# Second half of x turned inside the q/k product, two up units in side buffers, and the last y in another bank

## The chip, the core and the metric

One core of a Trainium2 chip runs the kernel. The metric is the device time of one execution in microseconds (us). The engines are TensorE (PE; PEld is its weight load), VectorE (DVE), ScalarE (ACT), GpSimd (POOL) and SyncE (SP). SyncE and ScalarE each issue transfers on a DMA queue of their own (q1 and q10 in the profile).

## The reference, cut to what matters

Two layers over 256 tokens of width 1024, all in float32. Layer 0 mixes with an mLSTM, layer 1 with windowed attention; each is followed by a grouped top-2 mixture of 16 experts and by layer norms.

```
proj = x @ w_in                      # q, k (512 each), v, o (1024 each), gates (2 x 4)
gates = 15 * tanh((gates + b_gates) / 15)
h = mlstm(q, k, v, gates) ; h = norm(h) * mh_norm * sigmoid(o) ; mix = h @ w_out
x = LN(alpha * x + mix)
for e in range(16):                  # moe, gate is zero but for the token's two experts
    g, u = split(t @ w_gu[e])        # 1024 -> 2 x 512
    out += gate[:, e] * ((silu(g) * u) @ w_down[e])
x = LN(alpha * x + out)
...                                  # layer 1: q, k, v, attention, w_out, LN, the same moe, LN
```

## The kernel before, in words

**Engines.** Every engine has its own program, written out in order; they meet only at semaphores. An instruction or a DMA issue that waits holds up everything behind it on its engine.

**Weights.** All large weights are streamed through `ring`, 22 slots of 1 MB ("units": 256 rows of a matrix, two a partition). Unit i goes into slot i modulo 22. SyncE issues the loads in the order of use; the load of unit i waits until `freed`, a counter that TensorE raises after its last use of each unit, has reached i - 21 (`free_slot`). TensorE waits for the slot's own counter (`need`). The q and k weights are units 0 to 3, then four each of v, o and w_out. From unit 16 on stand layer 0's experts: four up units (`u_gu`) and two down units (`u_dn`) each, in the order up(0), up(1), down(0), up(2), down(1) and so on; then the keys and values, q, w_out and the experts of layer 1.

**The start.** SyncE issues the first half of x's columns for both token tiles (two DMAs), unit 0, the second half of x (two DMAs), then units 1 and on. TensorE turns x in 128 x 128 blocks (`turn`, four blocks a call): both tiles of the first half (j=0), then both of the second (j=1). The copies of the results from PSUM to `hT` are divided: VectorE takes tile 1 of the first half, ScalarE the other three, in the order (tile 0, j 0), (tile 0, j 1), (tile 1, j 1). Then TensorE makes q and k transposed in one product, k = 0 to 7, with eight matmul instructions each (16 in the records, as each float32 matmul shows twice) into banks 0 to 3; k = 0 to 3 read the first half of x, k = 4 to 7 the second. Then come the gate product, which waits for `gates_w_in`, and the four V projections.

ScalarE loads the small parameters on its own queue, in its program order:

```
for t, j, n in ((0, 0, 1), (0, 1, 3), (1, 1, 4)):
    act.wait_ge(turned, n)
    A(hT[...], pb[4 + 2 * t + j]..., ACT.Copy).then_inc(hT_act, 1)
gate_weights()                       # four loads of w_in's gate columns, two of b_gates
act.dma_start(rows[0][0:4], ...)     # ln_g, ln_b, mh_norm, then w_rt x2, b_rt, sink x2, cs x2
...
for g in range(8):                   # only then q and k are copied out of PSUM, and the tanh follows
```

Each of the four loads of the gate columns moves 512 pieces of 16 bytes (four columns of 512 rows), each of the two bias loads four numbers. `gates_w_in` counts to 96 when all six are there; VectorE waits for it too, for its small operation on `b_gate` (in tile `misc`).

**The experts.** For expert u in `ORDER`, TensorE's `gate_up(u)` makes 64 token slots times 1024 columns in bank 0: 8 k steps of two matmul instructions, raising `freed` after each second k. ScalarE applies silu, VectorE multiplies and turns the result in 32 x 32 blocks (`turn_inner`, eight transposes) into `heT`. `down(u)` multiplies it by the two down units into bank 2, which VectorE and ScalarE must have emptied of the y before (`take_y`, counters `y_sb`). The order is gate_up(u+1), down(u), gate_up(u+2), down(u+1) and so on, with gathers (`gather`) and scatters (`scatter`) of tokens between for each quad of experts. The last quad ends: gate_up(15), down(14), a turn of the gate table (`turn_table`), down(15), scatter, layer norm.

Tile `bufA` holds the output gates of the mLSTM, the probabilities in layer 1, and in the experts the y of a quad, from the first `take_y` on. Tile `hT` holds turned activations, is read last before the experts by the routing product (which raises `logits`), and becomes the gathered tokens of the second quad.

Of the kernel before, what the change touches and what calls it, by code (L numbers as in the profile page):

```python
# [11 lines left out]
SEQ, D = 256, 1024  # L12
P = 128
NT = SEQ // P
# [23 lines left out]
TAKEN = 2.0e30  # L38
RING = 22
U_QK, U_V, U_O, U_WO = 0, 4, 8, 12  # L40
U_MOE = [16, 122]
U_KV, U_Q, U_WOB = 112, 114, 118


def u_gu(l, u):
    return U_MOE[l] + (6 * u - 2 if u else 0)


def u_dn(l, u):
    return U_MOE[l] + (6 * u + 8 if u < EXPERTS - 1 else 94)  # L50


def build(nc, x, w_in_a, b_gates_a, mh_norm_a, w_out_a, w_kv_shared, w_q_b, sinks_b, w_out_b,
          w_router, b_router, w_gu, w_down, ln_g, ln_b, rope, out):
    ctx = ExitStack()
    with ctx:
# [51 lines left out]
        probT = [bufA[:, 1024 + n * 512:1024 + (n + 1) * 512] for n in range(2)]  # L108

        res = gate_o  # L110
        ln_row = [bufB[:, n * D:(n + 1) * D] for n in range(2)]

        xe = [bufB[:, :].rearrange("p (k s) -> p k s", k=KC), hT]
# [42 lines left out]

        ring_in = [sem(f"ring_in{n}") for n in range(RING)]
        freed = sem("freed")
        x_in = [[sem(f"x_in{j}{t}") for t in range(NT)] for j in range(2)]
        gates_w_in, params_in = sem("gates_w_in"), sem("params_in")  # L160
        rows_in, rows_part, rows_ready = sem("rows_in"), sem("rows_part"), sem("rows_ready")
# [56 lines left out]
            return START + 14 * l + (4 * m - 2 if m else 0)  # L218


        SCB = [[[0, 1], [4, 5]], [[2, 3], [6, 7]]]
        SC_ORDER = [(t, par, jj) for t in range(NT) for jj in range(2) for par in range(2)]

        @block.sync
        def _(sp):
            def free_slot(i):

                if i >= RING:
                    sp.wait_ge(freed, i - RING + 1)
                if i == U_KV + RING:  # L230
                    sp.wait_ge(qT_done, 4)

            def load(i0, src):

                v = src.rearrange("(q p j) n -> p q j n", p=P, j=2)
                for q in range(src.shape[0] // 256):
                    buf, got = slot(i0 + q)
                    free_slot(i0 + q)
                    sp.dma_start(buf[:, :, :], v[:, q]).then_inc(got, 16)

            def load_down(i0, src):

                v = src.rearrange("(p q j) n -> p q j n", q=2, j=2)
                for q in range(2):
                    buf, got = slot(i0 + q)
                    free_slot(i0 + q)
                    sp.dma_start(buf[:, :, :], v[:, q]).then_inc(got, 16)

            def load_by_head(i0, src):

                v = src.rearrange("(k p) n -> p k n", p=P)
                for q in range(4):
                    buf, got = slot(i0 + q)
                    free_slot(i0 + q)
                    sp.dma_start(buf[:, :, :], v[:, 2 * q:2 * q + 2, :]).then_inc(got, 16)

            def spill(l):

                s = ov[l]
                sp.wait_ge(lists, l + 1)  # L260
                rounds = sp.value_load(extra[0:1, l:l + 1], min_val=0, max_val=3)
                with sp.If(rounds > 0):
                    sp.wait_ge(s["dve"], 1)
                    with sp.Fori(0, rounds) as j:
                        with sp.Fori(0, EXPERTS) as e:
                            n0 = (j * EXPERTS + e) * (KC + FC)
                            for k in range(KC + FC):

                                sp.wait_ge(s["w_used"], n0 + (k + START))
                                kk = k if k < KC else k - KC  # L270
                                if k < KC:
                                    src = w_gu[l, bass.ds(e, 1), kk // 2 * 256:(kk // 2 + 1) * 256, :].rearrange(
                                        "a (p j) n -> j (a p) n", j=2)[kk % 2]
                                else:
                                    src = w_down[l, bass.ds(e, 1), :, :].rearrange("a (p k) n -> k (a p) n", k=FC)[kk]
                                sp.dma_start(spill_w, src).then_inc(s["w_in"], 16)

            def load_x(j):

                for t in range(NT):  # L280
                    sp.dma_start(h[:, t, j * HALF:(j + 1) * HALF], x[0, t * P:(t + 1) * P, j * HALF:(j + 1) * HALF]).then_inc(x_in[j][t], 16)
            w_in = w_in_a[0]
            load_x(0)
            load(U_QK, w_in[0:256, 0:1024])
            load_x(1)
            load(U_QK + 1, w_in[256:1024, 0:1024])
            load(U_V, w_in[:, 1024:2048])
            load(U_O, w_in[:, 2048:3072])
            load(U_WO, w_out_a[0])
            load(u_gu(0, 0), w_gu[0, ORDER[0]])  # L290
            for l in range(2):
                for n, src in enumerate((ln_g, ln_b)):
                    sp.dma_start(norm_col[:, l, n, :].rearrange("p (a j) -> p a j", j=2),
                                 src[l, 0].rearrange("(a p j) -> p a j", p=P, j=2)).then_inc(cols_in, 16)
            for u in range(EXPERTS):
                if u + 1 < EXPERTS:
                    load(u_gu(0, u + 1), w_gu[0, ORDER[u + 1]])
                load_down(u_dn(0, u), w_down[0, ORDER[u]])
            for q in range(2):
                buf, got = slot(U_KV + q)  # L300
                free_slot(U_KV + q)
                sp.dma_start(buf[:, :, :].rearrange("p a (b n) -> p (a b) n", b=2).rearrange("p (a j) n -> p a j n", j=2),
                             w_kv_shared.rearrange("(a p j) n -> p a j n", p=P, j=2)[:, 2 * q:2 * q + 2]).then_inc(got, 16)
            load(U_Q, w_q_b[0])
            load_by_head(U_WOB, w_out_b[0])
            load(u_gu(1, 0), w_gu[1, ORDER[0]])
            load(u_gu(1, 1), w_gu[1, ORDER[1]])
            load_down(u_dn(1, 0), w_down[1, ORDER[0]])
            spill(0)
            for u in range(1, EXPERTS):  # L310
                if u + 1 < EXPERTS:
                    load(u_gu(1, u + 1), w_gu[1, ORDER[u + 1]])
                load_down(u_dn(1, u), w_down[1, ORDER[u]])
            spill(1)

            for t in range(NT):
                for c in range(2):
                    sp.wait_ge(ln_ready, 2 * (3 * NT + t) + c + 1)
                    sp.dma_start(out[0, t * P:(t + 1) * P, c * HALF:(c + 1) * HALF],
                                 h[:, t, c * HALF:(c + 1) * HALF]).then_inc(stored, 16)  # L320
            sp.wait_ge(stored, 16 * 2 * NT)
# [54 lines left out]
        def _(pe):  # L376
# [95 lines left out]


            pe.wait_ge(consts, NCONST)
            for j in range(2):
                for t in range(NT):
                    pe.wait_ge(x_in[j][t], 16)
                    turn(h, 0, t, j, 4)
            for k in range(KC):
                if k % 2 == 0:  # L480
                    need(U_QK + k // 2)
                if k % 4 == 0:
# [83 lines left out]
            def moe(l):  # L566
# [51 lines left out]
                def gate_up(u):  # L618
# [3 lines left out]
                    for k in range(KC):  # L622
                        if u and g == 0 and k == 4:
                            turn_table(m - 1)
                        if k % 2 == 0:
                            need(u_gu(l, u) + k // 2)
                        if g == 0 and k % 4 == 0:

# [5 lines left out]
                        for c in range(2):  # L634
                            last = mm(pb[0][c * 64:(c + 1) * 64, :].rearrange("p (a n) -> p a n", a=2),  # L635
                                      xe[m % 2][:, k, g * SLOTS:(g + 1) * SLOTS],
                                      slot(u_gu(l, u) + k // 2)[0][:, k % 2, :]
                                      .rearrange("p (a c n) -> p c a n", a=2, c=2)[:, c],
                                      start=k == 0, stop=k == KC - 1)
                        if k % 2:  # L640
                            last.then_inc(freed, 1)

                def turn_table(m):
# [8 lines left out]

                def down(u):
                    pe.wait_ge(heT_sb, E0 + (u + 1))
                    for t in range(NT):
                        pe.wait_ge(y_sb[t], (E0 + u) * 2 - START)
                    for hf in range(2):
                        w = slot(u_dn(l, u) + hf)[0]
                        need(u_dn(l, u) + hf)
                        for j in range(2):  # L660
                            for c in range(2):
                                last = mm(pb[2][c * 64:(c + 1) * 64, :],  # L662
                                          heT[u == EXPERTS - 1][:, (2 * hf + j) * 64:(2 * hf + j + 1) * 64],
                                          w[:, j, c * HALF:(c + 1) * HALF],
                                          start=(j, hf) == (0, 0), stop=(j, hf) == (1, 1))
# [222 lines left out]
        def _(act):  # L888
# [108 lines left out]
            def moe(l):  # L997
# [15 lines left out]
                def take_y(u):  # L1013
# [2 lines left out]
                    act.wait_ge(freed, u_dn(l, u) + 2)  # L1016
                    for t in range(NT):
                        A(ye[t][g * BLOCK:(g + 1) * BLOCK, HALF:2 * HALF],  # L1018
                          pb[2][64 + t * BLOCK:64 + (t + 1) * BLOCK, :], ACT.Copy).then_inc(y_sb[t], 1)

                def silu(u):
                    act.wait_ge(freed, u_gu(l, u) + 4)
                    A(act_g[u % 2], pb[0][:, 0:256], ACT.Silu).then_inc(silu_done, 1)  # L1023

                take_x(0, 0, 3)
# [101 lines left out]
        def _(dve):  # L1127
# [283 lines left out]
            def experts(l):  # L1411
# [16 lines left out]
                def take_y(u):  # L1428
# [2 lines left out]
                    dve.wait_ge(freed, u_dn(l, u) + 2)  # L1431
                    for t in range(NT):
                        V.tensor_copy(ye[t][g * BLOCK:(g + 1) * BLOCK, 0:HALF],  # L1433
                                      pb[2][t * BLOCK:(t + 1) * BLOCK, :]).then_inc(y_sb[t], 1)

                make_pick(0).then_inc(pick_ready, 1)
                V.reduce_max(extra_f[:, 0:1], pb[1][:, 32:64], AX_X)
# [229 lines left out]
```

## Time and profile before

| | |
|---|---|
| median of 3 runs | 689.04 us (688.61 to 690.35) |
| the profiled execution | 691.68 us, of which the span is 690.0 us |
| TensorE matmul, busy | 655.5 us (95%) |
| VectorE, busy | 284.3 us (41%) |
| ScalarE, busy | 139.7 us (20%) |
| bytes moved | 231.43 MB, mean 335 GB/s |
| chain that ended last | PE 81%, DMA 9%, DVE 5%, ACT 2% |

The profile is of one execution. Times in it count from the start of its span. A busy share is a mean over stages with different limits: the DMA engines are full for the first 86 us and during the experts (421 GB/s) and nearly idle between.

### The profile page before, as it was taken

The page shows a single profiled execution, that of the slowest core. Times are in us where ns is not written, and L with a number is a line of the kernel's source. Part 1 is how long each engine was busy: PE and PEld are TensorE (multiplying, and loading weights), DVE is VectorE, ACT ScalarE, POOL GpSimd, SP SyncE. Part 2 cuts the span into 40 slices and gives each one's busy share as a digit, 9 for nine tenths or more (in the row PEclk, how much of TensorE's full clock was granted, in tenths as well). Part 3 has the DMA queues.
Part 4 walks back from the last instruction along what each step waited for, and adds up shares of the span by engine and source line. Part 5 has one row for each costly group of instructions (what it writes and reads, how often), then busy time and mean ns, then how long its engine had stood idle before and what let it go on. Part 6 is the DMA issues. An engine that isn't in the chain of part 4 may idle for free.

```text
span 690.0 us, 7113 instructions
## 1 busy us (share of the span) xinstructions
PE 655.5 (95%) x2746; PEld 292.3 (42%) x2746; DVE 284.3 (41%) x730; ACT 139.7 (20%) x321; POOL 22.6 (3%) x41
## 2 busy tenths in 40 slices
PE   5999999999999999999979998999999999999974
PEld 4854564465333333333324454546333333333321
DVE  0001303256535335253445344456553444435356
ACT  1003234021121121121222042312021121021212
POOL 2040100000000000000000011200000000000000
PEclk9999999998999999999999999999999999999998
DMA  8999903261999999999999980823899999999991
GB/s 318 388 405 348 425 17 134 110 237 58 417 421 422 420 421 422 422 421 421 419 417 414 421 337 9 359 101 144 326 423 422 420 421 420 423 419 423 419 389 64
DMA packets 41431, 231.43 MB, mean 335 GB/s; under 512 B 10153, under 2 KB 10153, under 8 KB 15794
## 3 DMA queue, kind: packets, MB, share of 16 engines
q1 hardware_dynamic: 36960, 230.72, 81.7%
q10 hardware_dynamic: 4434, 0.21, 0.4%
q8 instruction: 24, 0.39, 0.2%
q14 instruction: 13, 0.11, 0.0%
HBM read 229.87 MB, written 1.05 MB: 335 GB/s over the span
## 4 chain that ended last, share of the span: by engine, by line
PE 81%; DMA 9%; DVE 5%; ACT 2%; SPq 1%; POOL 1%; issue 1%; POOLq 0%; DVEq 0%; ACTq 0%
PE pb L635 28%; PE pb L435 16%; PE pb L662 14%; DMA ring<-in_w_down 8%; PE pb L487 4%; PE pb L682 3%; PE pb L789 2%; PE pb L613 2%; PE pb L391 1%; PE pb L615 1%; PE pb L398 1%; PE pb L409 1%; DMA h<-in_x 1%; PE pb L538 1%; PE pb L579 1%; POOL bufA L372 1%
## 5 line engine op out<-in xcount | busy, mean ns | idle before, releaser
L435 PE MATMUL pb<-ring,hT 128*128 128x512 f32 x320 | 141.7, 595 | 0.8 <-DVE hT L1619 0.8
L662 PE MATMUL pb<-ring,bufC 128*64 128x512 f32 x512 | 117.0, 597 | 4.9 <-DVE bufA L1433 2.7
L635 PE MATMUL pb<-ring,hT 128*64 128x512 f32 x512 | 114.6, 594 | 2.0 <-DMA ring<-in_w_gu 2.0
L635 PE MATMUL pb<-ring,bufB 128*64 128x512 f32 x512 | 113.2, 593 | 0.0
L1407 DVE STREAM_TRANSPOSE bufC<-bufC 32x128 f32<-32x128 f32 x256 | 102.9, 402 | 3.8
L1433 DVE COPY bufA<-pb 32x512 f32<-32x512 f32 x64 | 43.7, 682 | 122.9 <-PE pb L662 121.9
L435 PEld LDWEIGHTS pb<-ring,hT 128*128 128x128 f32 x320 | 59.3, 190 | 69.7 <-issue 67.7
L635 PEld LDWEIGHTS pb<-ring,hT 128*64 128x64 f32 x512 | 36.0, 137 | 75.0 <-issue 68.0
L635 PEld LDWEIGHTS pb<-ring,bufB 128*64 128x64 f32 x512 | 36.2, 137 | 71.8 <-issue 70.0
L662 PEld LDWEIGHTS pb<-ring,bufC 128*64 128x64 f32 x512 | 35.0, 136 | 72.7 <-issue 68.1
L1018 ACT ACTIVATE bufA<-pb 32x512 f32<-32x512 f32 x64 | 37.7, 589 | 115.9 <-PE pb L662 115.1
L1023 ACT ACTIVATE bufC<-pb 128x256 f32<-128x256 f32 x32 | 12.3, 383 | 192.3 <-PE pb L635 192.3
L1416 DVE TENSOR_TENSOR bufC<-bufC,pb 128x256 f32<-128x256 f32 x32 | 13.5, 421 | 81.5 <-ACT bufC L1023 81.5
L682 PE MATMUL pb<-bufA,v_shift 128*128 128x512 f32 x64 | 29.5, 604 | 1.7 <-DVE bufA L1433 1.7
L487 PE MATMUL pb<-hT,ring 128*128 128x256 f32 x128 | 28.7, 387 | 0.0
L487 PEld LDWEIGHTS pb<-hT,ring 128*128 128x128 f32 x128 | 25.0, 196 | 3.5
L682 PEld LDWEIGHTS pb<-bufA,v_shift 128*128 128x128 f32 x64 | 11.5, 189 | 19.8 <-issue 19.8
L372 POOL TENSOR_TENSOR bufA<-bufA,st 128x512 f32<-128x512 f32 x8 | 8.1, 1039 | 357.8 <-DVE st L1608 357.8
L391 PE MATMUL pb<-ident,h 128*128 128x128 f32 x64 | 11.4, 324 | 8.0 <-DMA h<-in_x 7.7
L917 ACT ACTIVATE hT<-pb 128x512 f32<-128x512 f32 x12 | 6.7, 595 | 56.7 <-PE pb L391 56.7
L613 PEld LDWEIGHTS pb<-bufC,h 128*128 128x128 f32 x96 | 12.4, 208 | 9.7 <-issue 9.7
L789 PE MATMUL pb<-ring,hT 128*128 128x512 f32 x32 | 14.2, 596 | 1.1 <-ACT hT L917 1.1
(230 smaller groups left out, 430.0 us busy)
## 6 DMA issues: line engine op xcount, KB each, us to landing
ring<-in_w_gu SPq DMA_DIRECT2D x128, 1024.0 KB, 23.3
ring<-in_w_down SPq DMA_DIRECT2D x64, 1024.0 KB, 25.5
ring<-in_w_in_a SPq DMA_DIRECT2D x12, 1024.0 KB, 17.9
ring<-in_w_out_a SPq DMA_DIRECT2D x4, 1024.0 KB, 21.0
ring<-in_w_q_b SPq DMA_DIRECT2D x4, 1024.0 KB, 22.6
ring<-in_w_out_b SPq DMA_DIRECT2D x4, 1024.0 KB, 23.4
ring<-in_w_kv_shared SPq DMA_DIRECT2D x2, 1024.0 KB, 29.0
h<-in_x SPq DMA_DIRECT2D x4, 256.0 KB, 5.0
```

What stands on the lines that cost most here:

```text
L372: nc.gpsimd.tensor_tensor(p3, p3, st[:, o + 16:o + 20].rearrange("p (s o) -> p s o", o=1).to_broadcast([P, 4, P]), ALU.mult).then_inc(pn_r ...
L391: last = nc.tensor.transpose(pb[bank0 + 2 * t + j][:, kk * P:(kk + 1) * P], rows_of(src, t, k), ident[:, :])
L435: last = mm(pb[bank][:, :], hT[:, k, t * P:(t + 1) * P], slot(i0 + k // 2)[0][:, k % 2, c * HALF:(c + 1) * HALF], start=k == 0, stop=k == ...
L487: last = mm(pb[g // 2][:, (g % 2) * SEQ:(g % 2 + 1) * SEQ], slot(U_QK + k // 2)[0][:, k % 2, g * P:(g + 1) * P], hT[:, k, :], start=k == 0 ...
L613: last = nc.tensor.transpose(to, rows_of(h, t, k), table)
L635: last = mm(pb[0][c * 64:(c + 1) * 64, :].rearrange("p (a n) -> p a n", a=2), xe[m % 2][:, k, g * SLOTS:(g + 1) * SLOTS], slot(u_gu(l, u) ...
L662: last = mm(pb[2][c * 64:(c + 1) * 64, :], heT[u == EXPERTS - 1][:, (2 * hf + j) * 64:(2 * hf + j + 1) * 64], w[:, j, c * HALF:(c + 1) * H ...
L682: ins = mm(pb[4 + 2 * t + c][:, :], back[:, t * P:(t + 1) * P], ye[t][:, c * HALF:(c + 1) * HALF], start=False, stop=m == QUADS - 1, skip_ ...
L789: last = mm(pb[4 + t][:, :], hT[:, k, t * P:(t + 1) * P], kvw[:, k % 4, :], start=k == 0, stop=k == KC - 1)
L1018: A(ye[t][g * BLOCK:(g + 1) * BLOCK, HALF:2 * HALF], pb[2][64 + t * BLOCK:64 + (t + 1) * BLOCK, :], ACT.Copy).then_inc(y_sb[t], 1)
L1407: last = V.transpose(heT[to][q_out:q_out + 32, :].rearrange("p (k s) -> p k s", k=FC)[:, :, t * BLOCK:(t + 1) * BLOCK], act_g[n][q_in:q_in ...
L1433: V.tensor_copy(ye[t][g * BLOCK:(g + 1) * BLOCK, 0:HALF], pb[2][t * BLOCK:(t + 1) * BLOCK, :]).then_inc(y_sb[t], 1)
```

## The change

Three edits:

1. The start. TensorE turns the second half of x not ahead of the q/k product but between its steps k=2 and k=3 (`turn_x(1)`). Nothing changes in the programs of ScalarE and VectorE there, nor in SyncE's order.
2. Two up units of each layer's first expert (rows 512 to 1023 of its w_gu) don't go through the ring but into `bufA` and `hT` (`side`). SyncE issues them with the loads of experts 3 and 4, behind waits: `bufA`'s for the end of gating (layer 1: of attention), `hT`'s for the routing product. The first expert frees two slots in place of four; all later unit numbers move down by two in a layer.
3. The last expert's down product goes into bank 0 and doesn't wait for the y before to be taken from bank 2.

```diff
-U_MOE = [16, 122]
-U_KV, U_Q, U_WOB = 112, 114, 118
+U_MOE = [16, 120]
+U_KV, U_Q, U_WOB = 110, 112, 116
 def u_gu(l, u):
-    return U_MOE[l] + (6 * u - 2 if u else 0)
+    return U_MOE[l] + (6 * u - 4 if u else 0)
 def u_dn(l, u):
-    return U_MOE[l] + (6 * u + 8 if u < EXPERTS - 1 else 94)
+    return U_MOE[l] + (6 * u + 6 if u < EXPERTS - 1 else 92)
...
+        side = [bufA[:, :].rearrange("p (j n) -> p j n", j=2), hT[:, :, :].rearrange("p (j k) n -> p j (k n)", j=2)]
...
+        def y_bank(u):
+            return 2 if u < EXPERTS - 1 else 0
...
+            def load_side(l, n):
+                if n:
+                    sp.wait_ge(logits, l + 1)
+                elif l:
+                    sp.wait_ge(pv_done, 4)
+                else:
+                    sp.wait_ge(gated, 2)
+                sp.dma_start(side[n], w_gu[l, ORDER[0], (n + 2) * 256:(n + 3) * 256, :].rearrange("(p j) n -> p j n", j=2)
+                             ).then_inc(side_in[n], 16)
...
-            load(u_gu(0, 0), w_gu[0, ORDER[0]])
+            load(u_gu(0, 0), w_gu[0, ORDER[0], 0:HALF])
...
-                if u + 1 < EXPERTS:
+                if u == 3:
+                    load(u_gu(0, 4), w_gu[0, ORDER[4], 0:HALF])
+                    load_side(0, 1)
+                    load(u_gu(0, 4) + 2, w_gu[0, ORDER[4], HALF:D])
+                elif u + 1 < EXPERTS:
                     load(u_gu(0, u + 1), w_gu[0, ORDER[u + 1]])
+                if u == 2:
+                    load_side(0, 0)
                 load_down(u_dn(0, u), w_down[0, ORDER[u]])
...
-            for j in range(2):
+            def turn_x(j):
+
                 for t in range(NT):
                     pe.wait_ge(x_in[j][t], 16)
                     turn(h, 0, t, j, 4)
+
+            turn_x(0)
             for k in range(KC):
+                if k == 3:
+                    turn_x(1)
                 if k % 2 == 0:
                     need(U_QK + k // 2)
...
+                        apart = u == 0 and k >= 4
+                        w = (side[k // 2 - 2] if apart else slot(u_gu(l, u) + k // 2)[0])[:, k % 2, :]
+                        if apart and k % 2 == 0:
+                            pe.wait_ge(side_in[k // 2 - 2], 16 * (l + 1))
+                        elif k % 2 == 0:
                             need(u_gu(l, u) + k // 2)
...
-                        if k % 2:
+                        if u == 0 and k == KC - 1:
+                            last.then_inc(up0_done, 1)
+                        elif k % 2 and not apart:
                             last.then_inc(freed, 1)
...
-                    for t in range(NT):
-                        pe.wait_ge(y_sb[t], (E0 + u) * 2 - START)
+                    to = pb[y_bank(u)]
+                    if u < EXPERTS - 1:
+                        for t in range(NT):
+                            pe.wait_ge(y_sb[t], (E0 + u) * 2 - START)
```

The loads of layer 1 are edited like those of layer 0, `take_y` on both engines reads `y_bank(u)`, and silu of the first expert waits for `up0_done` in place of `freed`.

## Rows read from the trace of the kernel before

**Rows 1.** The chain of waits in order of time: start us, us, what.
```profile
11.60 28.47 PE pb L487 x128
40.07 3.58 PE pb L494 x16
...
641.11 27.57 DMA ring<-in_w_down
```

**Rows 2.** Timeline of DVE at 38 us (start us, us, operation, idle before).
```profile
38.38 0.14 DVE L1213 TENSOR_SCALAR misc<-misc 36x1 f32<-36x1 f32 x1 [32.06 <-DMA misc<-in_b_gates_a]
```

**Rows 3.** Timeline of PE, 341 to 360 us.
```profile
341.05 3.60 PE L635 MATMUL pb<-ring,hT 128*64 128x512 f32 x16
344.99 1.94 PE L635 MATMUL pb<-ring,hT 128*64 128x512 f32 x8 [0.34 <-DMA ring<-in_w_gu]
...
352.44 1.94 PE L662 MATMUL pb<-ring,bufC 128*64 128x512 f32 x8 [0.46 <-DMA ring<-in_w_down]
...
356.08 3.65 PE L662 MATMUL pb<-ring,bufC 128*64 128x512 f32 x16 [1.34 <-DVE bufA L1433]
```

**Rows 4.** Timeline of all engines, 0 to 16 us.
```profile
1.71 0.66 SPq L239 DMA_DIRECT2D ring<-in_w_in_a  x1
...
9.61 1.99 PE L391 MATMUL pb<-ident,h 128*128 128x128 f32 x8 [4.03 <-DMA h<-in_x]
```

**Rows 5.** DMA issues of the window 1.7 to 2 us (KB, us to landing).
```profile
ring<-in_w_in_a SPq DMA_DIRECT2D x1, 1024.0 KB, 7.2
```

**Rows 6.** PE by line: windows 12:12.5, 15:39; by stretch: PE busy, clock, DMA, GB/s.
```profile
L487 PE MATMUL pb<-hT,ring 128*128 128x256 f32 x3 | 1.5, 635 | 0.0
...
L487 PE MATMUL pb<-hT,ring 128*128 128x256 f32 x113 | 24.6, 379 | 0.0
...
11.40:13.40 2.00, 2.00 (x7) 1.00 1.03 422
154.00:157.80 3.80, 3.80 (x7) 0.50 0.39 166
```

**Rows 7.** Timeline of ACT and its DMA issues, 11 to 53 us.
```profile
11.65 1.02 ACTq L908 DMA_DIRECT2D v_shift<-in_w_in_a  x2
...
29.25 5.05 ACTq L938 DMA_DIRECT2D b_rt<-in_b_router  x1
...
42.24 10.15 ACTq L944 DMA_DIRECT2D cs<-rope  x2
```

**Rows 8.** Packets by queue (packets, MB, share), windows 14:22, 14:36, 22:36, 36:42 and 42:54.
```profile
q10 hardware_dynamic: 680, 0.01, 5.2%
...
q10 hardware_dynamic: 2077, 0.03, 5.8%
...
q1 hardware_dynamic: 1395, 5.39, 98.3%
...
q10 hardware_dynamic: 431, 0.06, 6.8%
...
q1 hardware_dynamic: 675, 4.90, 98.8%
q10 hardware_dynamic: 676, 0.04, 4.0%
```

**Rows 9.** DMA issues of the window 29.3 to 30 us.
```profile
b_rt<-in_b_router ACTq DMA_DIRECT2D x1, 8.0 KB, 30.2
```

**Rows 10.** Timeline of SyncE's DMA issues, 168 to 180 us.
```profile
168.81 5.48 SPq L239 DMA_DIRECT2D ring<-in_w_gu  x4
176.91 2.04 SPq L247 DMA_DIRECT2D ring<-in_w_down  x2
```

**Rows 11.** DMA issues of the windows 168.7:169 and 176.9:177.5.
```profile
ring<-in_w_gu SPq DMA_DIRECT2D x1, 1024.0 KB, 4.8
...
ring<-in_w_down SPq DMA_DIRECT2D x1, 1024.0 KB, 7.8
```

**Rows 12.** Timeline of DVE at 350 us.
```profile
350.32 3.29 DVE L1407 STREAM_TRANSPOSE bufC<-bufC 32x128 f32<-32x128 f32 x8
```

More of the change, by code:

```diff
@@ L158, in build @@
         freed = sem("freed")
+        side_in = [sem(f"side_in{n}") for n in range(2)]
+        up0_done = sem("up0_done")
         x_in = [[sem(f"x_in{j}{t}") for t in range(NT)] for j in range(2)]
@@ L305, in _ @@
             load_by_head(U_WOB, w_out_b[0])
-            load(u_gu(1, 0), w_gu[1, ORDER[0]])
+            load(u_gu(1, 0), w_gu[1, ORDER[0], 0:HALF])
             load(u_gu(1, 1), w_gu[1, ORDER[1]])
@@ L310, in _ @@
             for u in range(1, EXPERTS):
-                if u + 1 < EXPERTS:
+                if u == 3:
+                    load(u_gu(1, 4), w_gu[1, ORDER[4], 0:HALF])
+                    load_side(1, 1)
+                    load(u_gu(1, 4) + 2, w_gu[1, ORDER[4], HALF:D])
+                elif u + 1 < EXPERTS:
                     load(u_gu(1, u + 1), w_gu[1, ORDER[u + 1]])
+                if u == 2:
+                    load_side(1, 0)
                 load_down(u_dn(1, u), w_down[1, ORDER[u]])
@@ L624, in gate_up @@
                             turn_table(m - 1)
-                        if k % 2 == 0:
+                        apart = u == 0 and k >= 4
[3 more added lines that the diff above has]
+                        elif k % 2 == 0:
                             need(u_gu(l, u) + k // 2)
@@ L636, in gate_up @@
                                       xe[m % 2][:, k, g * SLOTS:(g + 1) * SLOTS],
-                                      slot(u_gu(l, u) + k // 2)[0][:, k % 2, :]
-                                      .rearrange("p (a c n) -> p c a n", a=2, c=2)[:, c],
+                                      w.rearrange("p (a c n) -> p c a n", a=2, c=2)[:, c],
                                       start=k == 0, stop=k == KC - 1)
-                        if k % 2:
+                        if u == 0 and k == KC - 1:
+                            last.then_inc(up0_done, 1)
+                        elif k % 2 and not apart:
                             last.then_inc(freed, 1)
@@ L661, in down @@
                             for c in range(2):
-                                last = mm(pb[2][c * 64:(c + 1) * 64, :],
+                                last = mm(to[c * 64:(c + 1) * 64, :],
                                           heT[u == EXPERTS - 1][:, (2 * hf + j) * 64:(2 * hf + j + 1) * 64],
@@ L1018, in take_y @@
                         A(ye[t][g * BLOCK:(g + 1) * BLOCK, HALF:2 * HALF],
-                          pb[2][64 + t * BLOCK:64 + (t + 1) * BLOCK, :], ACT.Copy).then_inc(y_sb[t], 1)
+                          pb[y_bank(u)][64 + t * BLOCK:64 + (t + 1) * BLOCK, :], ACT.Copy).then_inc(y_sb[t], 1)
                 def silu(u):
-                    act.wait_ge(freed, u_gu(l, u) + 4)
+                    if u:
+                        act.wait_ge(freed, u_gu(l, u) + 4)
+                    else:
+                        act.wait_ge(up0_done, l + 1)
                     A(act_g[u % 2], pb[0][:, 0:256], ACT.Silu).then_inc(silu_done, 1)
@@ L1433, in take_y @@
                         V.tensor_copy(ye[t][g * BLOCK:(g + 1) * BLOCK, 0:HALF],
-                                      pb[2][t * BLOCK:(t + 1) * BLOCK, :]).then_inc(y_sb[t], 1)
+                                      pb[y_bank(u)][t * BLOCK:(t + 1) * BLOCK, :]).then_inc(y_sb[t], 1)
                 make_pick(0).then_inc(pick_ready, 1)
```

## The prediction

> **What bounds the kernel now.** I read the page first: TensorE is busy 95% of the span, so what counts is where it waits and what it waits for. The chain of waits in order of time [rows 1] shows the first 44 us as TensorE alone: the q/k product from 11.60 us, then the gate product at 40.07 us with nothing between. At the end of each layer's experts the chain passes through a weight load instead (the second layer's, issued at 641.11 us, lands 27.57 us later). So three places matter: the start, the seam at 40 us, and the last two experts of each layer.
>
> At the seam the reader should ask by how much the gate product's own data is early. The gate weights and gate biases are loaded by ScalarE's DMA queue. VectorE waits for the same 96 counts, and starts at 38.38 us [rows 2]. The margin over TensorE's 40.07 is 1.7 us. That is all the slack the change may use up there.
>
> At the experts' end TensorE stalls four times because the loads arrive about 2.48 us apart (three steps from 344.99 to 352.44), while it eats a unit in about 1.75 us; then it waits 1.34 us for VectorE to empty the bank of the y before [rows 3].
>
> **Part 1, the second half of x.** What it gains: the q/k product need no longer wait for x's second half. TensorE starts those transposes at 9.61 us [rows 4]. It would start the product when its first weights are there: issued at 1.71 us, landing 7.2 us later, 8.9 us [rows 4, 5]. Full-speed cost of the product: 113 matmuls show in 24 us, 0.214 us each, 27.4 us for 128 [rows 6]; eight transposes take 1.99 us here, slow as the engine is after its idle time, so 1.0 us at full speed. From 9.61 to 40.07 are 30.46 us, so the restart after 4 us of idle time costs 30.46 - 27.4 - 1.0 = 2.1 us, of which I put 0.2 to the first matmul's fill and 1.9 to slow work: at 12 us a matmul still takes 635 ns against 379 ns later [rows 6]. The profile grants 1.00 (2.4 GHz) in this stretch and shows 0.50 (1.2 GHz) only elsewhere, as at 154 us [rows 6], so I read the slow level from the lengths alone. New end of the product: 8.9 + 27.4 + 1.0 + 1.9 = 39.2 us, 0.9 us earlier.
>
> What it moves: ScalarE's program order is three copies of turned x, then all its DMA issues. The second copy wants three turned tiles and the third four, and these now come before k=3 of the product. So everything ScalarE issues is late, the gate weights first. When: 8.9 us, three steps of k with 48 matmuls (10.3 us) and 1.9 us of slow start make 21.1; the transposes take 1.0 and the third copy starts behind the second, at about 22.3. Today the first issue comes as the transposes end, at 11.65 us [rows 4, 7]. So it comes about 10.7 us later. The gate loads took 38.38 - 11.65 = 26.7 us, because ScalarE's queue (q10) gets one packet for every packet of SyncE's weight queue (q1), which is full: 1395 against 2077 - 680 = 1397 from 22 to 36 us, and later 675 against 676 [rows 8]. While q1's packets are of 4 KB (the projection weights, rows of which are cut) that gives 100 packets a us; when they are of 8 KB it gives 676/12 = 56 [rows 8]. The gate loads are 2056 packets (four loads of 512 pieces of 16 bytes, and two of 4).
>
> Before: 2077 packets had gone by 36 us, 680 of them by 22 us, so the first went at about 15.2 us, 3.6 us after the issue, and the last at 35.8; the landing came 2.6 us behind. Now: first packet at 25.9 us. The 4 KB packets end at about 38 us whatever ScalarE does (12 units of 1 MB and x at 390 GB/s), and 12.2 us x 100 = 1220 packets go in that time. The 836 left go at 56 a us: 14.9 us, to 53.0 us. Behind it the landing lag of the 8 KB stretch: the bias row b_rt, about packet 3,230, was issued at 29.25 us and landed 30.2 us later, 59.5 [rows 7, 9]; 2077 + 431 + 676 = 3184 packets had gone by 54 us [rows 8], so packet 3,230 went at 54.8, a lag of 4.6 us. Landing now: 57.6 us. TensorE waits there from 39.2 us, with the whole V projection queued behind.
>
> Cost: 57.6 - 40.07 = 17.5 us, and TensorE starts slow again after an idle time longer than the 4 us before 9.61: the same 1.9 us. Sum **+19.4 us**. Bounds: below, the issue delay alone, as if the queue kept its pace (38.38 + 10.7 = 49.1 us, +9.0, and +1.9 makes +10.9); above, a lag of 3 us more and twice the slow start, +24.3. I take the packet count, since both rates are in the trace. Nothing queued later on ScalarE adds to it: its issues hold it until 52.4 us now (the load of `cs` [rows 7]), then q/k copies and tanh; in the new order about 62 to 71 us, and TensorE needs the tanh only before the fourth V projection, past 80 us. POOL's work on the norm rows follows the same queue and has the same cover.
>
> A page of the Trainium skill (DMA: Bandwidth & Descriptors, Queues, rings and completion order) says that each DMA engine goes round robin over the queues by whole packets, of typically 9 to 17 descriptors. If so, the gate loads would need a tenth as many turns, and the delayed issue would be hidden. The counts of [rows 8], one for one while both queues are full, speak against it for these loads.
>
> **Part 2, two up units in idle buffers.** Both side loads run while the DMA is idle or nearly (166 GB/s or less at 154 to 157.8 us [rows 6]): the bufA unit waits for gating, done before the second turn of val, long before the experts; the hT unit waits for the logits at 154 us and is wanted at k=6 of the first expert, about 171 us. In layer 2 the same distances hold. No cost. SyncE waiting for the logits holds only units that wait for the first expert anyway.
>
> The gain: 72 units instead of 74 go through the ring once experts start. But expert 0 now frees two slots, not four. Before, issues come at 168.81 us (four) and go on at 176.91 us [rows 10]; the load of 168.81 landed after 4.8 us, that of 176.91 after 7.8 us, at 184.7, as it queued behind others [rows 11]. In the new order the first two are done by then, and the issue of 176.91 meets an idle queue: 4.8 us, 181.7. The next step is then the starting one of 3.3 us in place of 2.5. Everything behind is 184.7 - 181.7 - 0.8 = **2.2 us** earlier, not two units' 4.97 us. Bounds 1.8 and 4.97.
>
> **Part 3, the last y in bank 0.** The last down product needs no emptied bank; its weights are two steps behind the landing of 352.44: 354.9 and 357.4 [rows 3]. Now, shifted by 2.2: expert 15's up part has no stall and ends at 341.05 + 6.9 = 348.0; down(14) waits for its second unit at 350.2 and ends 1.94 us later; the table 0.35; heT(15) is ready 4.2 us behind the up part (transposes end 353.61 where up ended 349.41 [rows 3, 12]), 352.2, in time. The last down's second unit lands at 355.2 and the product ends at 357.1, against 356.08 + 3.65 = 359.73. Gain 2.6 us. If the loads were the full 4.97 us earlier, the product would be bound by TensorE and heT: end 355.5, gain 4.2. If they were not earlier at all: 357.4 + 1.94 = 359.3, gain 0.4. Two layers: **-5.2 us**, bounds -0.8 and -8.4.
>
> **Sum.** Against the profiled execution's own 691.68 us (span 690.0): +17.5 + 1.9 - 5.2 = +14.2, so 705.9. The median shown is 2.64 us below it: 703.2.
>
> **Rivals.**
> A, the forecast above: 703.2 us, own range 698 to 708. Chance 0.68.
> B, the queue keeps its pace and only the 10.7 us of delay count: +10.9 - 5.2 = +5.7, 694.7. For it: 26.7 us is the only time seen for these loads. Against it: the two rates of [rows 8]. Chance 0.15.
> C, the other side: the gate loads land within 16.9 us of their issue, before the product ends at 39.2 (few packets, ahead of the weights once they run). Then the start gives 0.9 us and the experts 5.2: 682.9, faster. The kernel stays faster for any landing up to about 43 us (40.07 + 5.2 - 1.9), 21 us after the issue. Against it: 26.7 us in this trace. By the skill's packets of many descriptors it would be this one. Chance 0.06.
> D, the shifted load stream gives the experts nothing (the gap after expert 0 eats both units): -0.8 in place of -5.2, 707.6. For it: 8.1 us between the issues of [rows 10] against four units' 9.9. Chance 0.11.
>
> **Numbers.** 0.3% (2 us) is about what a measurement of this kernel tells from no change. Slower: A, B, D: 0.94. Same: a landing near 43 us, 0.01. Faster 0.05. The range takes A and D and B's value: 694 to 709.
>
> **What the profile would show.** Right: DVE's small operation on misc at about 57 us, in place of 38.38; TensorE idle from 39 us until then, released by ScalarE's loads; its first matmuls after it slow; the gate load's issue at about 22 us; a short idle stretch of the DMA near 175 us of the old time; the last down of each layer released by a load and not by a y copy. Wrong: the seam at 40 us closed, or the experts' end with TensorE never waiting. The prediction fails if the small loads run faster than one packet per weight packet, or if ScalarE issues them before its second copy.

## The result and the profile after

703.27 us median (700.38 to 705.49, 4 runs) against 689.37 (688.61 to 690.35, 4 runs): ratio 1.020, 95% interval 1.016 to 1.024. The kernel became slower by 13.9 us; 703.2 was forecast. The profiled execution took 703.88 us, span 702.2, against 691.68 and 690.0: 12.2 us more. (The profiled execution of the kernel before is slower than all four runs of its median, so the two differences aren't the same.)

The chain of waits of the changed kernel, in order of time (start us, us, what), answers to [rows 1]:

```profile
1.71 7.20 DMA ring<-in_w_in_a
8.95 12.86 PE pb L522 x48
...
30.37 25.21 DMA misc<-in_b_gates_a
55.62 6.43 PE pb L529 x16
62.05 27.68 PE pb L465 x64
```

The seam between the q/k product and the gate product at 40 us, closed before, now holds a wait. TensorE's chain leads to ScalarE's last gate load, issued at 30.37 us, and the gate product starts at 55.62 instead of 40.07. It then takes 6.43 us instead of 3.58. Why the load is late shows in the timeline of ScalarE:

```profile
22.32 0.60 ACT L971 ACTIVATE hT<-pb 128x512 f32<-128x512 f32 x1 [16.96 <-PE pb L421]
22.80 0.45 ACTq L950 DMA_DIRECT2D v_shift<-in_w_in_a  x1
...
30.37 3.46 ACTq L952 DMA_DIRECT2D misc<-in_b_gates_a  x1
```

The second copy of x waited 16.96 us for TensorE's transposes; the first gate load stands behind it, at 22.80 us against 11.65 [rows 7]. The timeline of VectorE gives the landing, 55.60 against 38.38 [rows 2]:

```profile
55.60 0.15 DVE L1258 TENSOR_SCALAR misc<-misc 36x1 f32<-36x1 f32 x1 [48.90 <-DMA misc<-in_b_gates_a]
```

The slow gate product is in TensorE by stretches (length, busy, granted clock, DMA share, GB/s):

```profile
40.00:44.00 4.00, 0.03 (x1) 1.00 1.04 413
44.00:48.00 4.00, 0.00 (x0) 0.53 1.01 402
...
56.00:58.00 2.00, 2.00 (x6) 0.50 0.03 1
58.00:60.00 2.00, 2.00 (x6) 0.50 0.38 122
60.00:62.00 2.00, 2.00 (x8) 0.67 0.95 380
```

TensorE has nothing to do from 40.03 us on. The granted clock is 1.00 (2.4 GHz) in the stretch to 44 us, 0.53 in the mean of the next, still 0.50 (1.2 GHz) from 56 to 60 us, where the gate product runs, and 0.67 in the mean of the stretch from 60 to 62 us, in which it returns.

The end of layer 0's experts, in the timeline of TensorE, answers to [rows 3]:

```profile
359.74 7.04 PE L674 MATMUL pb<-ring,hT 128*64 128x512 f32 x32
366.90 1.94 PE L704 MATMUL pb<-ring,bufC 128*64 128x512 f32 x8
369.32 1.94 PE L704 MATMUL pb<-ring,bufC 128*64 128x512 f32 x8 [0.48 <-DMA ring<-in_w_down]
...
371.89 1.94 PE L704 MATMUL pb<-ring,bufC 128*64 128x512 f32 x8 [0.27 <-DMA ring<-in_w_down]
374.32 1.94 PE L704 MATMUL pb<-ring,bufC 128*64 128x512 f32 x8 [0.49 <-DMA ring<-in_w_down]
377.14 3.67 PE L724 MATMUL pb<-bufA,v_shift 128*128 128x512 f32 x8 [0.88 <-DVE bufA L1478]
```

The last up part has no stall, the wait for the y is gone, and three loads still come late: the last down is bound by its loads, as forecast. From expert 1's up part (174.97 us before, 193.67 now, in the chain) to the last scatter (360.60, 377.14) the layer now takes 183.47 us in place of 185.63: 2.2 us gained. Layer 1: 490.86 to 676.89 before, 505.84 to 689.10 now, 186.03 against 183.26: 2.8 us.

The books of the span: wait for the gate loads +15.55; slow gate product +2.85; small differences up to expert 1 of layer 0 +0.3; layer 0's experts -2.16; between them and expert 1 of layer 1 -1.56; layer 1's experts -2.77; sum +12.2. The -1.56 was in no step of the forecast. It is mostly the gathers ahead of layer 1's experts: 32 records in 5.37 us before and 3.84 us now. The clock granted there was 0.65 before and 1.00 now:

```profile
478.00:482.00 4.00, 4.00 (x25) 0.65 0.02 4
```
```profile
494.50:498.50 4.00, 4.00 (x32) 1.00 0.02 4
```

(The first is of the kernel before, the second of the changed one.) The change isn't the reason. In the twelve traces of this case the chain shows these gathers at 5.36 or 5.37 us in four (before, e2, e9, e10) and at 3.84 us in eight, and kernels of either kind stand on both sides: e6, whose start is that of the kernel before, has 3.84.

### The profile page after: what moved, and what is told of

Its sections match the earlier page's. It is cut to its first block, busy times and chain, and to the rows that moved or that the text cites. A ratio compares the mean times of both kernels' runs of the same rounds, so it can differ in the third digit from the quotient of the medians.

```text
span 702.2 us, 7111 instructions
## 1 busy us (share of the span) xinstructions
PE 657.3 (94%) x2746; PEld 292.0 (42%) x2746; DVE 284.3 (40%) x730; ACT 140.0 (20%) x321; POOL 22.6 (3%) x41
## 4 chain that ended last, share of the span: by engine, by line
PE 76%; DMA 13%; DVE 5%; ACT 2%; ACTq 1%; POOL 1%; issue 1%; POOLq 0%; SPq 0%; DVEq 0%
PE pb L674 28%; PE pb L465 16%; PE pb L704 13%; DMA ring<-in_w_down 8%; PE pb L724 4%; DMA misc<-in_b_gates_a 4%; PE pb L831 2%; PE pb L648 2%; PE pb L522 2%; PE pb L421 1%; PE pb L650 1%; DMA ring<-in_w_in_a 1%; PE pb L573 1%; PE pb L439 1%; ACTq L950 1%; PE pb L529 1%
## 5 line engine op out<-in xcount | busy, mean ns | idle before, releaser
L465 PE MATMUL pb<-ring,hT 128*128 128x512 f32 x320 | 142.0, 596 | 0.8 <-DVE hT L1664 0.8
L674 PE MATMUL pb<-ring,bufB 128*64 128x512 f32 x480 | 106.4, 594 | 0.0
L674 PEld LDWEIGHTS pb<-ring,bufB 128*64 128x64 f32 x480 | 33.9, 137 | 67.2 <-issue 65.4
L522 PE MATMUL pb<-hT,ring 128*128 128x256 f32 x128 | 30.3, 401 | 3.0 <-DMA ring<-in_w_in_a 3.0
L529 PE MATMUL pb<-hT,v_shift 128*36 128x256 f32 x16 | 6.4, 591 | 15.6 <-DMA misc<-in_b_gates_a 15.6
```

The costliest lines, as they stand in the source:

```text
L465: last = mm(pb[bank][:, :], hT[:, k, t * P:(t + 1) * P], slot(i0 + k // 2)[0][:, k % 2, c * HALF:(c + 1) * HALF], start=k == 0, stop=k == ...
L522: last = mm(pb[g // 2][:, (g % 2) * SEQ:(g % 2 + 1) * SEQ], slot(U_QK + k // 2)[0][:, k % 2, g * P:(g + 1) * P], hT[:, k, :], start=k == 0 ...
L529: last = mm(pb[4][0:GW, 0:SEQ], w_gate[:, k, :], hT[:, k, :], start=k == 0, stop=k == KC - 1)
```

## The experiments

Each kernel starts from the changed one or from the one before, as said. "To scatter" is the time from expert 1's up part to the last scatter of a layer in the timeline of TensorE, layer 0 / layer 1: in the kernel before 185.7 / 186.1 us, in the changed one 183.5 / 183.3.

How far can one such time be trusted? Eight traces tell, of kernels whose experts' code is the same. The experts of the kernel before took 185.7 / 186.1 us there and 185.5 / 184.7 in e2. Those of the changed kernel took 183.5 / 183.3 there, 184.4 / 184.2 in e1, 183.5 / 184.3 in e3, 183.7 / 184.1 in e8, 183.5 / 183.6 in e9 and 184.3 / 183.7 in e10. One layer differs by up to 1.4 us from one execution to the next. The means are 185.5 and 183.8 us: the change's parts 2 and 3 give 1.6 us a layer, 3.3 us in both.

**e1_turn_first: part 1 undone.**

```diff
             turn_x(0)
+            turn_x(1)
             for k in range(KC):
-                if k == 3:
-                    turn_x(1)
```

> The changed kernel with the second half of x turned ahead of the product again, the two side units and the last y's bank kept. My theory (the delayed gate loads cost the start, the experts gain): gate landing back at about 38 us, no wait at the seam, so before minus the experts' gain of 2.2 and 2.8 us seen in the changed kernel: 684.4 us, ratio 0.993. Rival (side loads or bank do harm of their own somewhere): above 687. If the slow start of the changed kernel is not from the turning: about 700.

686.09 us median (12 runs) against 689.37 (20 runs), ratio 0.995, interval 0.993 to 0.997. The gate loads are issued at 10.39 us, land at 37.34, and TensorE doesn't wait at the seam. To scatter: 184.4 / 184.2, 1.3 and 1.9 us gained. The whole loss is part 1's; the other two parts give 3.3 us by the medians, with 1.9 to 4.5 as the interval, and 3.3 by the means above.

**e2_turn_only: part 1 alone, on the kernel before.** The same loop as in the change, nothing else.

> The kernel before with nothing but the second half of x turned between k=2 and k=3. My theory: the gate loads are issued at about 22.4 us and land late. With SyncE's order as before, the small loads of norm_col stand two weight units later in its queue than in the changed kernel; if it is these that let the gate loads through 2 us earlier there (55.6 against my 57.6), they land here at 57 to 58 us. Time: 40.07 to 57.5 and some 2.9 us of slow matmuls, so before + 20: 709 us. Rival (the landing doesn't depend on the other queue's packets): 55.6 us again, 707. Rival (most of the loss is in the experts' part): under 700.

708.51 us (4 runs), ratio 1.027, interval 1.024 to 1.031. Issue 23.12 us, landing 58.30:

```profile
58.30 0.15 DVE L1218 TENSOR_SCALAR misc<-misc 36x1 f32<-36x1 f32 x1 [51.58 <-DMA misc<-in_b_gates_a]
```

That is 2.7 us later than in the changed kernel with an issue only 0.3 later. What differs is SyncE's queue. The change cuts the first expert's loads there to two units, and `norm_col`, thousands of packets of 4 bytes, comes two units sooner. The packets of the window 50 to 54 us, changed kernel first, then e2 (packets, MB, share):

```profile
q1 hardware_dynamic: 1162, 1.20, 88.7%
q10 hardware_dynamic: 1024, 0.08, 23.7%
```
```profile
q1 hardware_dynamic: 227, 1.65, 100.2%
q10 hardware_dynamic: 227, 0.00, 3.6%
```

Where 4-byte packets stand among q1's large ones, q10's come through at 256 a us instead of 57. So the change's part 2 gave part 1 back some 2.7 us of its harm, by way of a queue's order. No run moves `norm_col` alone, but e8 and e9, with SyncE's order of the changed kernel, have loads of 32.5 and 33.1 us, near its 32.8 and not e2's 35.2.

**e3_gates_early: the cause removed.** The changed kernel, with the gate loads issued behind ScalarE's first copy.

```diff
             for t, j, n in ((0, 0, 1), (0, 1, 3), (1, 1, 4)):
+                if n == 3:
+                    gate_weights()
                 act.wait_ge(turned, n)
...
-            gate_weights()
             act.dma_start(rows[0][0:4], ln_g.rearrange("l w n -> (l w) n")).then_inc(rows_in, 16)
```

> The changed kernel with ScalarE's gate loads issued behind its first copy of x, before the copies that now wait for k=3. My theory: issue at about 5.4 us, landing at or under 33 us, no wait at the seam, the q/k product ends at about 40 us (22.6 + 17.4), nothing gained at the start against before, the experts' 5 us kept: 684 us. Rival (the wait is moved to the loads behind, the norm rows or the copies of q and k): ScalarE's q/k copies would be late past 62 us and the fourth V projection waits; above 688. If order on ScalarE is not the cause: 703.

685.58 us (9 runs), ratio 0.993, interval 0.991 to 0.996. Issue 4.79, landing 32.08 us; ScalarE's q and k copies start at 40.15, earlier than before. With x still turned in the middle the loss is gone: the turning is harmless, ScalarE's order does it. The chain:

```profile
1.71 7.37 DMA ring<-in_w_in_a
9.12 12.36 PE pb L522 x48
21.49 0.95 PE pb L421 x8
22.44 17.27 PE pb L522 x80
39.71 3.57 PE pb L529 x16
```

The gate product starts at 39.71, 0.4 us before its old time of 40.07. That isn't shown to be a gain: in the timelines of the five kernels with x turned first it starts between 38.4 (e1) and 41.0 us (e5), 40.0 in the mean, and in e3 and e7 at 39.6 and 39.3. What turning inside the product is worth, about half a us at most, is less than these executions differ by.

**e4_side_second: part 2 at another place.** As e1, with the side buffers for expert 1's last two up units.

```diff
-    return U_MOE[l] + (6 * u - 4 if u else 0)
+    return U_MOE[l] + (6 * u - 4 if u > 1 else 4 * u)
...
-                sp.dma_start(side[n], w_gu[l, ORDER[0], (n + 2) * 256:(n + 3) * 256, :]...
+                sp.dma_start(side[n], w_gu[l, ORDER[1], (n + 2) * 256:(n + 3) * 256, :]...
...
-                        apart = u == 0 and k >= 4
+                        apart = u == 1 and k >= 4
```

> As e1, but the two side buffers take the last two up units of the second expert, not of the first. The first expert then frees four slots as before and the load stream has a queue of work when the two missing ones come. My theory (the idle time of the DMA behind expert 0 eats most of the two units' 4.97 us): no idle stretch there, the last units land a full 4.97 us earlier, no stall by loads in the last experts; end 1.6 us a layer before e1's: 681.2 us. Rival (the shift was lost elsewhere, in issue or bandwidth): the same as e1, 684.4.

682.77 us (6 runs), ratio 0.991, interval 0.988 to 0.993. To scatter: 182.0 / 181.9, 3.7 and 4.1 us gained against the trace before, 3.5 and 3.5 against the mean of 185.5. The end of layer 0's experts has no wait for a load any more:

```profile
339.87 7.04 PE L675 MATMUL pb<-ring,hT 128*64 128x512 f32 x32
346.73 3.60 PE L705 MATMUL pb<-ring,bufC 128*64 128x512 f32 x16
...
351.17 3.65 PE L705 MATMUL pb<-ring,bufC 128*64 128x512 f32 x16 [0.47 <-DVE bufC L1453]
```

What is left is 0.47 us for heT, the bound that the forecast gave for loads a full 4.97 us early. In the changed kernel the DMA engines do stand still behind expert 0's two freed slots (by stretches, all engines; the last two numbers are DMA share and GB/s):

```profile
192.00:194.00 2.00, 2.00 (x8) 0.49 (x6) 0.98 (x3) 0.38 (x1) 0.00 (x0) 1.00 0.98 401
194.00:195.00 1.00, 1.00 (x8) 0.32 (x6) 0.96 (x4) 0.00 (x0) 0.00 (x0) 1.00 0.32 123
195.00:196.00 1.00, 1.00 (x8) 0.40 (x6) 0.97 (x3) 0.00 (x0) 0.00 (x0) 1.00 0.00 0
196.00:197.00 1.00, 1.00 (x6) 0.28 (x4) 0.94 (x4) 0.00 (x0) 0.00 (x0) 1.00 0.66 115
```

In e4 the share is 1.01 from 170 to 184 us, and then 0.77 to 0.88 until 190: a dip, but no standstill.

**e5_side_only and e6_bank_only: parts 2 and 3 apart.** e5 is e1 with `y_bank` always 2 and the wait restored; e6 is the kernel before with the last down product and its y in bank 0.

> The side units alone: x turned first, the last y in bank 2 with its wait. My theory: the loads come 1.8 to 2.2 us earlier, down(14) ends that much earlier, then the wait for the y (1.34 us) and down(15) at full speed: 2.0 us a layer, before - 4: 685.4 us. If the bank alone makes e1's gain: 689.

> The kernel before with the last y in bank 0 alone. My theory: the last down's second unit lands only at 357.4, so the 1.34 us wait for the y turns into a wait for loads and 0.4 us a layer are left: 688.6 us, no difference that can be measured. Rival (the y's wait was the bound): 1.3 us a layer, 686.7.

e5: 686.70 us (12 runs) against 689.40 (23 runs), ratio 0.996, interval 0.994 to 0.999; to scatter 184.0 / 184.6, so 1.7 and 1.5 us gained; the wait for the y is there in full, 1.33 us, which is as expected. e6: 687.52 us (12 runs), ratio 0.998, interval 0.996 to 1.000; to scatter 184.9 / 184.6, 0.75 and 1.5 us; the wait for the y has turned into waits for loads:

```profile
353.88 1.94 PE L667 MATMUL pb<-ring,bufC 128*64 128x512 f32 x8 [0.28 <-DMA ring<-in_w_down]
356.27 1.94 PE L667 MATMUL pb<-ring,bufC 128*64 128x512 f32 x8 [0.45 <-DMA ring<-in_w_down]
```

e6's median lies between my 688.6 and the rival's 686.7 and doesn't decide. The waits show that loads and not the y now hold the last down product. How much the bank alone gives is not shown: e2, which has neither part 2 nor part 3, gained 0.2 and 1.4 us by the same reckoning, as much in layer 1 as e5 and e6. The layer times of e4 and e7, which wait for no load there, agree within 0.1 us.

**e7_all: e3 and e4 together,** with x's second half turned inside the product.

> Gate loads early (e3) and side units at the second expert (e4), with x's second half turned in the product and the last y's bank. Theory: the experts' gain of e4 (3.7 and 4.1 us by its trace) with at most 0.4 us at the start: 681.5 us, level with e4's 682.8 within the noise. Rival (the two add up with something of the turning): under 681.

682.54 us (6 runs), ratio 0.991, interval 0.988 to 0.995, level with e4. With e4 the best of the versions; to scatter 182.0 / 182.0.

**e8_awake and e9_awake_17: the slow restart.** The changed kernel with idle matmuls in the wait for the gate loads, 34 and then 17.

```diff
+            stay_awake(6, 17)
             pe.wait_ge(gates_w_in, 96)
```

> The changed kernel with 34 idle matmuls of 128x512 (14.7 us at full speed) in TensorE's wait for the gate loads. Theory: the landing of the loads stays at 55.6 us, the gate product then takes 3.6 us in place of 6.43, so 700.4 us. Rival (the slow gate product isn't from the idle time): 703.3, gate product at 6.4 us.

> As e8_awake, whose filler took 29.5 us since each idle matmul shows twice (0.43 us a record): now 17 of them, 14.7 us, ending just ahead of the gate loads' landing at about 55 us. Theory: the landing unchanged, the gate product in 3.6 us, 2.8 us less than the changed kernel: 700.5 us. Rival: no difference, 703.3.

e8 missed its point: the filler ran 29.5 us and held the product up itself (717.68 us, ratio 1.043); I had counted one record a matmul. e9: 701.39 us (4 runs), ratio 1.019, interval 1.014 to 1.024; the changed kernel's own ratio is 1.020, so the total doesn't tell. The timeline does:

```profile
40.35 14.82 PE L428 MATMUL pb<-ident 128*128 128x512 f32 x34
56.43 3.64 PE L530 MATMUL pb<-hT,v_shift 128*36 128x256 f32 x16 [1.26 <-DMA misc<-in_b_gates_a]
```

The gate product takes 3.64 us against 6.43 and the granted clock is 1.00 throughout, while the landing (56.41) stays late: the 2.8 us are the price of the idle time. The price doesn't grow in step with that time. In e2 TensorE was idle for 17.98 us and its gate product took 5.48 us, 1.9 more than at full speed; in e10 it was idle for 5.29 us and paid 1.5:

```profile
58.32 5.48 PE pb L499 x16
```
```profile
45.69 5.04 PE L529 MATMUL pb<-hT,v_shift 128*36 128x256 f32 x16 [5.29 <-DMA misc<-in_b_gates_a]
```

What differs is where the clock comes back: in e2 it is 0.98 in the stretch from 62 to 64 us, in the changed kernel 0.67 from 60 to 62, though its product started 2.7 us sooner.

**e10_turn_at_k1: a smaller delay.** The changed kernel with `if k == 1` in place of `if k == 3`.

> The changed kernel with the second half of x turned before k=1 in place of k=3: two steps of k, 6.8 us, earlier. ScalarE's first issue at about 15.5 us. Pure delay (the loads take 26.7 us wherever they start): landing 42.2 us. My packet count (first packet 3.6 us behind the issue, 100 a us until 38 us, 56 after): 1910 packets by 38.2, the other 146 by 40.8, landing 44 to 45.4 us with a lag between 2.6 and 4.6 us. TensorE waits 5 to 6 us; time before + 4.5 + about 2 of slow matmuls - 4: 691 to 692 us by the packet count, 689 by pure delay.

694.74 us (6 runs) against 689.73 (11 runs), ratio 1.009, interval 1.006 to 1.013. Issue 16.27 us, landing 45.67, 29.4 us later. That is 2.7 us beyond pure delay, as the packet count has it; q10 sent 1888 packets from 18 to 40 us, while q1 sent 2110. The time itself came out 3 us above what I wrote. The V projection starts at 50.66 us, 7.0 later than before, of which I had counted 6.5. The rest of the gap stays open. The profiled execution (693.58 us) is 1.9 us above that of the kernel before, and what I had written adds up to 2.5; it is the other runs, up to 697.2 us, that lift the median.

The issue, landing and duration of the gate loads in all twelve traces, in order of issue:

| kernel | issue us | landing us | duration us |
|---|---|---|---|
| e7_all | 4.70 | 32.58 | 27.9 |
| e3_gates_early | 4.79 | 32.08 | 27.3 |
| e1_turn_first | 10.39 | 37.34 | 26.9 |
| e4_side_second | 11.31 | 37.95 | 26.6 |
| e5_side_only | 11.64 | 38.84 | 27.2 |
| before | 11.65 | 38.38 | 26.7 |
| e6_bank_only | 11.73 | 38.34 | 26.6 |
| e10_turn_at_k1 | 16.27 | 45.67 | 29.4 |
| e8_awake | 22.67 | 55.16 | 32.5 |
| changed | 22.80 | 55.60 | 32.8 |
| e2_turn_only | 23.12 | 58.30 | 35.2 |
| e9_awake_17 | 23.29 | 56.41 | 33.1 |

Loads that run wholly in the time of q1's 4 KB packets take 26.6 to 27.9 us; the later they start, the more of them meets 8 KB packets.

## Why the prediction was right

**The moved step.** That ScalarE's issues wait behind copies that wait for k=3 was right: the first issue came at 22.80 us, forecast 22.3. e3 shows it as the cause: only the issue's place differs from the changed kernel, and 703.3 becomes 685.6.

**The length of the loads.** The landing came at 55.60 us, forecast 57.6. The two rates are right; e2, which has SyncE's order of before, lands at 58.30, 0.7 us from the working. The term that was off: I left SyncE's queue as it was, though the change takes two units out ahead of `norm_col`, and small packets in q1 speed up q10. Rival B (pure delay, 49.1 us) falls by the table. Rival C (few turns for the gate loads) falls too: wherever both queues had work, packets went one for one, up to `norm_col`. The Trainium skill (DMA: Bandwidth & Descriptors, Queues, rings and completion order) says that an engine goes round the queues by whole packets and that a packet typically holds 9 to 17 descriptors. The turns are borne out: 445 packets of ScalarE's queue for 446 of SyncE's from 42 to 50 us in the changed kernel. Packets of many pieces are not: 680 packets of ScalarE's queue from 14 to 22 us held 0.01 MB [rows 8], some 16 bytes or one piece each, and it is the measurement that decides.

**The restart.** 2.85 us for 1.9, with twice the 1.9 as a bound. The term was taken from a restart after 4 us of idle time. A longer wait isn't shown to be the reason for the difference: e2 paid 1.9 us after 18.0 us of idle time. In the changed kernel the clock granted was 0.50 until 60 us, 4.4 us into the product.

**The start.** The product's end: 22.60 + 17.43 = 40.0 us for 39.2, since its first 48 matmuls took 12.86 us for 12.2. All of it is hidden behind the wait for the gate loads. Where that wait is gone, in e3 and e7, the 0.9 us that the forecast gave this step isn't seen beyond the spread between executions.

**The experts.** In the two profiled executions -2.2 and -2.8 us for -2.6 each, but that agreement is luck. This is the term that was mis-sized: over the four layers with the old experts and the twelve with the changed ones the gain is 1.6 us each, and by e1's medians 3.3 us in all (1.9 to 4.5), where the forecast had 5.2. The mechanism was right: idle time of the DMA behind expert 0, and most of two units' gain lost there, of which e4 gives much back by feeding the queue. Rival D (no gain beyond 0.8 us) falls with e1, whose interval excludes it, though the measured gain lies about halfway between D and the forecast. The 0.4 us for the bank alone is neither shown nor refuted by e6.

**The sum.** +12.2 in the profiled span for +14.2: gate wait 1.95 less, restart 0.95 more, small differences up to the experts 0.3 more, the experts' gain 0.3 smaller, and 1.6 less in the gathers of layer 1, by the clock granted there. Medians differ by 13.9. That the median fell within 0.1 us of 703.2 is luck: by the medians of the changed kernel and of e1, part 1 cost 17.2 us for 19.4 and the other parts gave 3.3 for 5.2, so that two misses of about 2 us cancel, and the runs of the changed kernel spread over 5 us.

## What to carry to other kernels

Where a step is moved in one engine's program, follow the semaphore that it raises to the other engines and look at what stands behind the waits there: here a queue of small DMA issues behind a 0.6 us copy cost more than everything the change could gain. A load of many small pieces beside a full queue is priced in packets, not in bytes, and its time depends on the packet size of the queue beside it. A buffer added to a stream loses much of its worth where the stream then runs dry: take the slots away where transfers are already queued, not from the first consumer (3.5 us a layer in e4 against 1.6). And before a difference of 1 us between two traces is put down to a change, compare traces in which that code is the same.

## What the runs showed of the hardware

Two DMA queues that both had work shared the engines packet for packet: with weight packets of 4 KB in the one (3860 bytes in the mean) the other got 100 a us, and with those of 8 KB (7260 in the mean) 56. With 4-byte packets mixed in, it got 256 a us from 50 to 54 us of the changed kernel (1024 packets beside 1162). TensorE's granted clock was 0.50 from 48 us on in the wait of 15.6 us and the product behind it took 2.85 us more, which 14.8 us of idle matmuls avoided; behind waits of 18.0 and 5.3 us in other kernels it was 1.9 and 1.5 us. The gathers of layer 1 took 5.37 or 3.84 us, with a clock of 0.65 or 1.00 granted there in the two traces looked at: 1.5 us between executions whose work in that stretch is the same. And the clock granted over a whole execution goes with its time in one and the same kernel: of the 23 runs of the kernel before beside e5, the three under 687 us had 0.990 or 0.991, the others, 687.7 to 692.0 us, 0.982 to 0.987.
